# Weight sets of the first groups of an MLP stage, and the order of VectorE's jobs, in a three-layer transformer kernel

## The reference, cut to what matters

```python
# first block
z = rms_norm(x, norm_mix) @ w_in
...
x = x + merged @ w_out
h2 = rms_norm(x, norm_mlp)
x = x + square(relu(h2 @ w_up)) @ w_down          # width 4096
x = rms_norm(x, norm_final)
# second block, twice
x = x + 0.5 * swiglu(rms_norm(x, ffn1_norm), wg, wu, wd)   # width 2816
z = rms_norm(x, mix_norm) @ w_in
...
x = x + concatenate([attn_out, conv_out]) @ w_out
x = x + 0.5 * swiglu(rms_norm(x, ffn2_norm), wg, wu, wd)
# at the end
x = rms_norm(x, final_norm)
```

## Time and profile before

| | |
|---|---|
| median of 3 runs | 2504.76 us (2504.3 to 2505.38) |
| profiled execution, its own time | 2501.46 us |
| its span in the trace | 2499.3 us |
| mean granted clock of TensorE in it | 0.989 |

### The profile page before, as it was taken

How to read it: one execution, slowest core, us unless ns; L and a number is a source line. 1 busy time by engine, 2 the same in 40 slices (tenths; PEclk the granted TensorE clock), 3 DMA queues, 4 the chain that set the end, 5 groups by cost and what they waited for, 6 DMA issues and landing times.

```text
span 2499.3 us, 36547 instructions
## 1 busy us (share of the span) xinstructions
PE 2427.9 (97%) x14620; PEld 2158.8 (86%) x14620; DVE 1822.6 (73%) x2639; ACT 1269.4 (51%) x2023; POOL 195.3 (8%) x199
## 2 busy tenths in 40 slices
...
GB/s 204 151 124 126 118 135 85 102 102 100 100 71 79 107 102 102 68 106 156 109 84 95 102 102 102 98 89 93 102 102 77 109 152 110 85 102 102 102 101 68
DMA packets 103640, 263.76 MB, mean 106 GB/s; under 512 B 9648, under 2 KB 12976, under 8 KB 103088
## 3 DMA queue, kind: packets, MB, share of 16 engines
...
## 4 chain that ended last, share of the span: by engine, by line
PE 73%; DVE 12%; ACT 6%; issue 5%; DMA 3%; POOL 1%; SPq 0%; POOLq 0%; DVEq 0%; ACTq 0%
PE bank L1107 12%; PE bank L1108 12%; PE bank L1109 12%; PE bank L1155 12%; PE bank L1156 11%; PE bank L1157 11%; DVE w_raw_lo L1600 2%; DVE slot_lo L1600 2%; DVE x L1864 1%; ACT w_hi L1315 1%; PE bank L1171 1%; PE bank L1186 1%; DMA w_raw<-w_out_dram 1%; DVE rms_inv L1760 1%; ACT z L1303 1%
## 5 line engine op out<-in xcount | busy, mean ns | idle before, releaser
L1361 ACT ACTIVATE slot_hi<-slot_raw 128x1024 fp32r<-128x1024 f32 (+1 forms) x396 | 365.2, 952 | 144.3 <-DVE slot_raw L1646 115.8
L1600 DVE TENSOR_TENSOR slot_lo<-slot_raw,slot_hi 128x1024 fp32r<-128x1024 f32 (+1 forms) x396 | 427.1, 1100 | 4.1 <-ACT slot_hi L1361 4.1
L1155 PE MATMUL bank<-hs_hi,slot_hi 128*128 128x256 f32 x1504 | 426.1, 283 | 0.1
L1157 PE MATMUL bank<-hs_hi,slot_lo 128*128 128x256 f32 x1504 | 426.2, 283 | 0.0
L1156 PE MATMUL bank<-hs_lo,slot_hi 128*128 128x256 f32 x1504 | 426.1, 283 | 0.0
L1107 PE MATMUL bank<-act_hi,w_hi 128*128 128x512 f32 x960 | 380.3, 396 | 7.8 <-DVE w_raw_lo L1600 7.8
L1108 PE MATMUL bank<-act_lo,w_hi 128*128 128x512 f32 x960 | 380.2, 396 | 0.0
L1109 PE MATMUL bank<-act_hi,w_raw_lo 128*128 128x512 f32 x960 | 374.6, 390 | 0.0
L1155 PE MATMUL bank<-h_hi,slot_hi 128*128 128x256 f32 x1128 | 322.8, 286 | 39.2 <-DVE slot_lo L1600 35.8
L1379 ACT ACTIVATE part_a<-bank 128x256 f32<-128x256 f32 x188 | 71.8, 382 | 531.0 <-PE bank L1157 530.4
L1864 DVE SCALAR_TENSOR_TENSOR x<-bank,x 128x512 f32<-128x512 f32 x280 | 192.3, 687 | 191.3 <-PE bank L1109 190.0
...
## 6 DMA issues: line engine op xcount, KB each, us to landing
slot_raw<-ffn_wg_dram SPq DMA_DIRECT2D x88, 512.0 KB, 4.1
slot_raw<-ffn_wu_dram SPq DMA_DIRECT2D x88, 512.0 KB, 4.1
w_raw<-ffn_wd_dram SPq DMA_DIRECT2D x88, 512.0 KB, 3.7
w_raw<-w_in_dram SPq DMA_DIRECT2D x67, 512.0 KB, 3.6
w_lo<-w_raw POOLq DMA_DIRECT2D x43, 512.0 KB, 4.7
slot_raw<-w_up_dram SPq DMA_DIRECT2D x32, 512.0 KB, 4.4
w_raw<-w_down_dram SPq DMA_DIRECT2D x32, 512.0 KB, 3.6
w_raw<-w_out_dram SPq DMA_DIRECT2D x24, 512.0 KB, 3.7
```

The lines of the kernel that those rows point to most:

```text
L1155: engine.matmul(to, slot_hi[:, g % 2, slot, lhs], hi, start=opens, stop=False, skip_group_check=True)
L1157: product = engine.matmul(to, slot_lo[:, g % 2, slot, lhs], hi, start=False, stop=closes, skip_group_check=True)
L1361: engine.activation(span_of(slot_hi, n, name), span_of(slot_raw, n, name), ACT.Copy).then_inc(signals["s_hi"].s, 1)
L1600: engine.tensor_tensor(lo, value, hi.bitcast(F32), ALU.subtract).then_inc(signals[event].s, 1)
```

## The change

1. **Sets.** Both plain groups of a stage are in one set, which needs its seven slots and an eighth block of 128x512: this lies in the last quarter of the buffers of mixed h (`hs_raw`, `hs_hi`, `hs_lo`), named `lead_x`. The third group has the other set to itself. Its load and its preparation no longer wait for the plain groups. In the output projection all loads of the first three groups are issued behind the first unit, and the groups are prepared from units 2, 3 and 4 on. From one MLP to the next the third group is loaded and prepared during the last Strassen groups, and the plain groups at the end of the last one.
2. **Third mix.** As `hs_hi` and `hs_lo` of j = 3 hold the eighth block, `mix_hi` of j = 3 waits for the first half of the first plain group, and this mix stands two slots later.
3. **Scaled squares.** The seven additions into `scaled_sum` go from GpSimd to VectorE (job `scaled_add`).
4. **Low parts.** `h_lo` becomes a job of its own (`h_rest`) two slots behind `h_tile`; `split_rest` stands three slots behind the unit's high part, not two.

```diff
-PLAIN_PARTS = {"plain_a": (B11, 2), "plain_b": (B22, 2)}
-PARTS.update(PLAIN_PARTS)
-PLAIN_SLOT = ((B11, B21), (B12, B22))
+LEAD_SLOTS = (((0, None), (2, 4)), ((1, 6), (3, 5)))
+LEAD_PARTS = (("lead_a", (0, 3, 2)), ("lead_b", (4, 5, 1))), (("lead_a", (1, 4, 2)), ("lead_b", (5, 7, 1)))
...
-            self.later(2, "split_rest", u)
+            self.later(3, "split_rest", u)
...
+        self.later(2, "h_rest", s, m)
...
-                self.add("scaled", (s, m), None, self.z("scaled_sum", (s, m)))
+                self.scaled_z[m] = self.z("scaled_sum", (s, m))
+                self.add("scaled", (s, m), None, self.scaled_z[m])
+                self.later(3, "scaled_add", s, m)
...
-            if m < 2:
-                self.load("a", n + m)
-                self.load("b", n + m)
-            elif m == 2:
-                self.prepare_ahead(0)
+            if m == 0:
+                for part, ahead in (("a", 0), ("b", 0), ("x", 0), ("a", 1), ("b", 1), ("a", 2), ("b", 2)):
+                    self.load(part, n + ahead)
+            elif 2 <= m < 4:
+                self.prepare(n + m - 2, 0)
+            elif m == 4:
+                self.prepare(n + 2, 0, 3)
...
+    def set_of(self, n):
+        return 1 - n % 2 if self.sg[n].lead == 0 else n % 2
+
+    def in_set_before(self, n):
+
+        lead = self.sg[n].lead
+        before = n - 1 if lead == 0 else n - 2 if lead == 1 or self.sg[n - 2].lead != 0 else n - 4
+        return None if n in self.block_of else before
...
+    def loads_when(self, g, what):
+
+        group = self.sg[g]
+        ahead = self.sg[g + 1].lead if g + 1 < self.block_end else None
+        if group.lead == 0:
+            if what == "end":
+                self.load("a", g + 3)
+        elif group.lead == 1:
+            if what == "half":
+                self.load("b", g + 2)
+        elif ahead == 0:
+            if what == "P6":
+                self.load("a", g + 1)
+            elif what == "end":
+                for part, n in (("b", g + 1), ("x", g + 1), ("a", g + 2), ("b", g + 2)):
+                    self.load(part, n)
+        elif what in ("P6", "end"):
+            n = g + 4 if g + 2 < self.block_end and self.sg[g + 2].lead == 0 else g + 2
+            self.load("a" if what == "P6" else "b", n)
...
+        self.was_prepared.add(n)
+        if self.sg[n].lead == 0:
+            steps = ((0, "s_hi", (n, "lead_a")), (1, "s_hi", (n, "lead_b")), (2, "s_hi", (n, "lead_x")),
+                     (2, "s_lo", (n, "lead_a")), (3, "s_lo", (n, "lead_b")), (4, "s_lo", (n, "lead_x")))
+        elif self.sg[n].lead == 1:
+            steps = ((0, "s_hi", (n, "lead_a")), (2, "s_hi", (n, "lead_b")), (2, "s_lo", (n, "lead_a")), (4, "s_lo", (n, "lead_b")))
...
-            self.later(slots + after, job, *key)
+            self.later(slots + pace * after, job, *key)
...
-        assert self.prepared > g
-        if self.prepared == g + 1 and g + 1 < self.block_end:
-            self.prepare(g + 1)
+        assert g in self.was_prepared
+        if not group.plain:
+            if g + 1 < self.block_end and self.sg[g + 1].lead == 0:
+                self.prepare(g + 3)
+            else:
+                self.prepare(g + 1, 2 if self.sg[g - 1].lead == 1 else 8)
...
-        order = [(n, k) for n in range(2) for k in range(KT - 2)] + [(n, k) for n in range(2) for k in (KT - 2, KT - 1)]
-        if self.pending_norm is not None:
+        order = [(n, k) for n in range(2) for k in range(KT)]
+        if group.lead == 0:
+            order = [(n, k) for n in range(2) for k in range(KT - 2)] + [(n, k) for n in range(2) for k in (KT - 2, KT - 1)]
             for j in range(1, HALF_K):
-                self.mix(group.stage, j, 6 * (j - 1) + 2)
+                self.mix(group.stage, j, (2, 8, 16)[j - 1])
...
-        self.prepare_ahead(4)
+        self.prepare(self.groups_done, 5)
+        self.prepare(self.groups_done + 1, 9)
...
+                    if j == HALF_K - 1:
+                        act.wait_ge(*done("p_mm", (plan.lead_of[s], 0)))
...
+                elif job == "scaled_add":
+                    v.wait_ge(*done("scaled_squared", key))
+                    if key[1] > 1:
+                        v.wait_ge(*done("scaled_sum", (key[0], key[1] - 1)))
+                    engine.tensor_tensor(scaled_sum[:, :], scaled_sum[:, :], z[plan.scaled_z[key[1]] % Z_RING][:, :],
+                                         ALU.add).then_inc(signals["scaled_sum"].s, 1)
```

More of the change, by code:

```diff
@@ L146, with plain @@
     order: tuple
-    plain: bool
+    lead: int | None
+    @property
+    def plain(self):
+        return self.lead is not None
 class Plan:
@@ L646, in plain @@
         self.sz1[g] = self.z(*used)
-        self.load("a", g + 2)
-        self.load("b", g + 2)
+        self.loads_when(g, "end")
         self.grouped()
@@ L929, in span_of, with lead_weights, landed_part, set_was_free @@
         def span_of(t, n, name):
-            first, count = PARTS[name]
-            if name in PLAIN_PARTS:
-                return t[:, n % 2, first:first + 2 * count - 1:2, :]
-            return t[:, n % 2, first:first + count, :].rearrange("p a n -> p (a n)")
+            lead = plan.sg[n].lead
+            if name == "lead_x":
+                return {"slot_raw": hs_raw, "slot_hi": hs_hi, "slot_lo": hs_lo}[t][:, :, HALF_K - 1, 0:P]
+            t = {"slot_raw": slot_raw, "slot_hi": slot_hi, "slot_lo": slot_lo}[t][:, plan.set_of(n)]
+            if lead is not None:
+                first, last, step = dict(LEAD_PARTS[lead])[name]
+                return t[:, first:last:step, :]
+            first, count = PARTS[name]
+            return t[:, first:first + count, :].rearrange("p a n -> p (a n)")
+        def lead_weights(g, n, k):
+            slot = LEAD_SLOTS[plan.sg[g].lead][n][k % 2]
+            j = k // 2
+            if slot is None:
+                return hs_hi[:, j, HALF_K - 1, 0:P], hs_lo[:, j, HALF_K - 1, 0:P], "lead_x"
+            part = "lead_a" if k % 2 == 0 else "lead_b"
+            return slot_hi[:, plan.set_of(g), slot, j * P:j * P + P], slot_lo[:, plan.set_of(g), slot, j * P:j * P + P], part
+        def landed_part(part, n):
+            return done(plan.landing(part, n), n)
+        def set_was_free(engine, n, slot, products):
+            before = plan.in_set_before(n)
+            if before is None:
+                return
+            if plan.sg[before].plain:
+                engine.wait_ge(*done("p_mm", (before, slot)))
+            else:
+                for product in products:
+                    engine.wait_ge(*done("s_mm", (before, product)))
         def group_source(n):
```

144 lines of the change are left out of this document (85 added, 59 removed).

## The result

The changed kernel takes 2489.65 us (median of 4 runs, 2488.99 to 2491.94) against 2505.07 of the kernel before (4 runs): ratio 0.994, 95% interval 0.9927 to 0.9952. It is 15.4 us faster; the forecast was 35 us. The profiled execution took 2488.99 us, with a span of 2487.2. One run of the study, of the later mix in experiment 7, was slow (2935.18 us at a granted clock of 0.751) and is left out of its median.

The account below looks back on a forecast made before the run. TensorE, busy 97% of the span, was taken as the bound, with gains only where it waits or runs at the lower clock. Third groups -31, loads +3, down-projection ends -7 make -35 us: 2504.76 to 2470, range 2456 to 2490.

Parts of the forecast that it names:

- Rival (c): At the third groups and fourth products the stall only moves: 5 us kept at each of four places, 2489 us; chance 0.15.
- What bounds the kernel: TensorE, busy 97%, waits 34.96 us at five third groups, whose weights are prepared late because they share a set.
- The loads: In the output projections, seven loads issued together delay the next w_out: 1 us at each of three, 3 us in all.
- Rival (b): The loads starve the output projection, 3 us at each of three: 2476 us; chance 0.1.
- The preparation in the output projection: 6.7 us more VectorE work there fits its idle time; taken as 0, upper bound 1.7 us at each of three.
- `part_b`: Behind the plain groups P4 waits for ScalarE's copy of P7: 1.5 us at four places, 5 us at stage 2.
- The ends of the down projections: Two TensorE stalls on w_raw_lo ahead of a stage; w_raw_lo ahead of h_lo takes away two thirds, -7 us.
- The scaled squares: Seven sums moved from GpSimd to VectorE: 4.8 us in, 0 to 7.6 us out, about nothing in sum.
- Rival (a): VectorE's seven adds collide with GpSimd's square adds and stage 2 stays late: gain 22 us, 2483 us; chance 0.15.
- The small pieces: 18 more instructions on ScalarE and VectorE for the split first group, hidden in idle time; without that cover 7 us.
- The signs: Profile marks: TensorE idle falling under 20 us means (a) or (c); output-projection waits on w_raw_lo or DMA growing, (b) or (d).
- (d): VectorE becomes the bound in the output projections and the kernel gets slower: 2510 us; chance 0.05.

Follow-up runs that it names:

- experiment 7: Changed kernel, one edit each: w_hi sooner at the down projections' last units, 2498.77 us; first mix four slots later, 2493.91; second plain group's preparation later, 2487.89.
- experiment 1: Changed kernel with the seven loads issued behind units 0, 1 and 2 of the output projection in place of all behind unit 0: 2475.99 us.
- experiment 3: Changed kernel with the seven scaled sums back on GpSimd: 2489.51 us.
- experiment 4: Changed kernel with ScalarE's copy part_b ahead of the second plain group's act_hi and the next group's slot_hi: 2480.5 us.
- experiment 5: Changed kernel with h_lo at once: 2512.5 us; with parts 3 and 4 undone: 2511.19, with loads in portions too: 2495.89; kernel before with part 4 alone: 2493.36.

## Why the prediction was wrong

The time lies just under the upper bound of the range, 2490, but the gain is 15.4 us where 35 was forecast. Rival (c) has the number, 2489, by luck: it kept 5 us at each of four places, where 1.7 to 2.9 are measured, and knew nothing of the loads, which are the largest part of what is missing. By the steps of the prediction:

**What bounds the kernel: right.** The third-group stalls, their place and their cause hold; all 34.96 us of them are gone, and the third group of stage 4 begins at once behind the plain ones (1272.03).

**The loads: the step that failed most clearly.** It took 1 us at each of three output projections, at most 3; the loads cost 13.7 us in all (experiment 1), some 4.6 each. That is 10.7 of the 19.6 us by which the gain fell short. The step counted 3 MB at 353 GB/s, 9 us, and forgot what shares the queue: the `w_out` tile asked for just ahead and the late tile itself, 4 MB in all; that these make the difference is argued. It said 3.6 us late with 4.8 to spare; measured is 335.44 - 329.27 = 6.2 us late, and 6.2 - 4.8 = 1.4 is near the first stall, 1.62. And it stopped at the first late tile, while `w_raw_lo`, `x` and the next `w_hi` follow it on two engines in order (337.82 and 344.88 both wait). Rival (b) named the mechanism, with a chance of 0.1.

**The preparation in the output projection: "I take 0" has the number right and the reason wrong.** With the new order the preparation costs TensorE nothing there (in experiment 1 it is busy 60.00 of 60 us at stage 1, and has no wait on `w_raw_lo` at the others). But the step counted VectorE's idle time, 2.31 in 10 us, as room. Part of that is 0.79 us for `h_hi` in each unit, in which an engine in order can do nothing else. By the old order the norm's sum is late by 2.3 us at each output projection (7.0 on `sum_lo`), over the step's bound of 1.7, and `w_raw_lo` is late besides; the new order turns the wait for `h_hi` into room. The step was saved by part 4, of which it says nothing. Order and sets are not two terms of a sum:

| | old order | new order |
|---|---|---|
| sets of before | 2505.07 | 2493.36 |
| sets of the change | 2511.19 | 2489.65 |
| sets of the change, loads in three portions | 2495.89 | 2475.99 |

(The left column lacks part 4. Part 3, which experiment 3 found to be worth nothing, is only in the two lower kernels of the right column.) The prediction gave the sets -28 us net and the order -7. Measured, the sets are +6 to +8 by themselves and -4 to -5 with the order; the order is -10 to -12 by itself and -20 to -24 with the sets.

**`part_b`: right in mechanism, too small.** Forecast were 6 us at four stages and 5 at stage 2, 11 in all; measured 14.1 (2.90, 6.12 and three times 1.7) and 3.2 on `hs_lo` of the third mix, which the sum had left out. The chain comes to 5.5 - 4.4 = 1.1, which the step wrote as 1.5; 1.7 is measured. Of the 9.5 us of low clock 7 were to come back. At stages 1 and 2 the new waits bring the low clock again, for 3.41 and 5.85 us; by the prediction's own reckoning these lose 3.41 - 15 x 0.122 = 1.6 and 5.85 - 27 x 0.122 = 2.6, so some 5 came back. In all, experiment 4 gives 9.2 us of this part back.

**The ends of the down projections: -7 in the forecast, about -1 measured.** The order alone does bring what was forecast, and more (experiment 5). With the whole change these stalls stand again at 3.41 and 2.07, 1.7 less than before, and the low clock behind them costs 5.44 - 13 x 0.244 = 2.3 and 3.42 - 9 x 0.244 = 1.2, where it was 2.7 in sum. Not the slots of `w_hi`, nor the mix, nor by itself the second plain group's preparation is the cause (7). In the changed kernel both plain groups are prepared in these last units, where before one was done earlier; that this is the cause is argued, not shown, and the third group's preparation in the last Strassen groups was not tested apart. The order has a price too: the longer waits on `square_sum` and on `z` in the later mixers (3.2 and 3.2) are there with the order alone (2.5 and 3.3), and shorter with `h_lo` at once (1.9 and 1.0).

**The scaled squares: right**, nothing in sum. The seven sums take VectorE 8.9 us, not 4.8 (1.27 each), yet its busy time fell, from 1822.6 to 1817.3. Rival (a) is out: with the sums on GpSimd the time is the same. Yet a piece of the earlier trace rows's kind is seen in the output projections, where preparation now meets GpSimd's squares (`h_lo` 1.78 in place of 0.75 above). That was in no term. The Trainium skill ("SBUF — State Buffer", section "Who interferes with whom") says that a VectorE instruction with two inputs in SBUF contends with GpSimd's reads; `h_lo` at 1.78 agrees. What it costs in sum no run here tells.

**The small pieces: right as nothing**, though the page counts one more instruction a stage on each of the two engines (2023 to 2028 on ScalarE; 2639 to 2651 on VectorE with the seven sums), 10 and not 18.

**The signs: one right, one misleading.** A rise of L1107's waits on `w_raw_lo` inside the output projections was to mean (b) or (d), and it shows: about 7 us in single waits of 1.3 to 1.6, where none of that size stood, and a `w_hi` that waited 6.82 for its DMA. That the idle time fell by less than 20 us (by 6.8) was to mean (a) or (c); (c) is a part of it, the loads are more.
